# Sample attention's indexer, key and value pages: first loads issued in the last mixer steps, keys and values from two queues

## What is computed

```python
def dsa_sample(q, k, v, qi, ki, wi, cache_k, cache_v, cache_ki, page_table):
    ...
    ki_past = cache_ki[page_table].reshape(Bn, past, IDX_DIM).astype(ki.dtype)
    ki_all = jnp.concatenate([ki_past, ki], axis=1)
    ...
    score = index_scores(qi, wi, ki_all)
    score = jnp.where(kpos[None, None, :] <= qpos[None, :, None], score, -jnp.inf)
    _, top_i = lax.top_k(score, topk)
    ...
    kg = jnp.where(is_new, take(k, new_i), cache_k[phys, off].astype(k.dtype))
    vg = jnp.where(is_new, take(v, new_i), cache_v[phys, off].astype(v.dtype))
    return sparse_attend(q, kg, vg, valid)
```

## Time and profile before

| what | value |
|---|---|
| median of 3 runs (lowest, highest) | 4593.22 us (4589.61, 4599.74) |
| profiled execution, its own time | 4589.05 us |
| its span in the trace | 4587.4 us |
| PE, DVE, ACT, POOL busy | 81%, 47%, 23%, 12% |
| sample phase of layer 0, loading of `sel` to the end of its last store | 996.2 to 1326.7 us |
| the same of layer 1 | 3287.1 to 3618.0 us |

### The profile page before, as it was taken

One profiled execution on the slowest core, in us unless ns is written; L12 is line 12 of the kernel. 1 busy time (PEld: TensorE's weight loads), 2 busy tenths in 40 slices (PEclk: granted clock), 3 DMA queues, 4 the chain that ended last, 5 costly groups with the idle time before them and its releaser, 6 DMA issues.

```text
span 4587.4 us, 52594 instructions
## 1 busy us (share of the span) xinstructions
PE 3712.4 (81%) x17978; PEld 2757.6 (60%) x17978; DVE 2138.1 (47%) x4901; ACT 1037.1 (23%) x2273; POOL 546.9 (12%) x767
## 2 busy tenths in 40 slices
PE   5787778776638999999957787787766389999999
PEld 3555455553324899989835554554433248899898
DVE  1357788715503344344413577787155033443443
ACT  2322333223300211112022333332233002111120
POOL 0100100114120000100001000001141201001000
PEclk9888877556769999999978888775567699999999
DMA  3000000015331111111130000000153311111111
GB/s 121 19 13 14 14 10 8 7 29 168 98 130 60 46 37 56 37 37 56 44 120 20 12 13 15 10 8 7 30 170 96 128 60 47 37 56 37 37 56 49
DMA packets 165855, 230.68 MB, mean 50 GB/s; under 512 B 64562, under 2 KB 130164, under 8 KB 163540
## 3 DMA queue, kind: packets, MB, share of 16 engines
q1 hardware_dynamic: 139892, 166.03, 11.0%
q0 software_dynamic: 25696, 61.29, 4.4%
HBM read 203.74 MB, written 23.50 MB: 50 GB/s over the span
## 4 chain that ended last, share of the span: by engine, by line
PE 62%; issue 11%; DVE 10%; SPq 5%; ACT 4%; DVEq 2%; DMA 2%; POOLq 2%; POOL 1%; ACTq 0%
PE bank L1302 11%; PE bank L1303 11%; PE bank L1304 11%; PE bank L1012 9%; PE bank L1008 4%; PE bank L1110 3%; PE bank L1294 3%; DVE arena L1363 3%; SPq L455 2%; SPq L471 2%; ACT arena L642 1%; PE bank L1094 1%; POOLq L591 1%; DVE arena L1629 1%; SPq L424 1%
## 5 line engine op out<-in xcount | busy, mean ns | idle before, releaser
L1771 DVE TENSOR_TENSOR x_and_hraw<-x_and_hraw,bank 128x512 f32<-128x512 f32 (+1 forms) x576 | 396.4, 688 | 630.6 <-PE bank L1304 630.6
L642 ACT ACTIVATE arena<-bank 128x512 f32<-128x512 f32 (+11 forms) x926 | 356.2, 428 | 1112.6 <-PE bank L1012 335.8
L1012 PE MATMUL bank<-arena 128*128 128x512 f32 (+5 forms) x1440 | 526.3, 521 | 3.5 <-ACT arena L669 2.0
L1363 DVE TENSOR_SCALAR_CACHE_REDUCE arena<-arena,vectors 128x384 bf16<-128x384 f32 (+6 forms) x434 | 500.2, 1152 | 34.4 <-issue 2.5
L1302 PE MATMUL bank<-xT_hi,w_up_hi 128*128 128x364 f32 (+1 forms) x1536 | 506.7, 330 | 3.2 <-DVE vectors L1752 3.2
L1303 PE MATMUL bank<-xT_lo,w_up_hi 128*128 128x364 f32 (+1 forms) x1536 | 506.6, 330 | 0.0
L1304 PE MATMUL bank<-xT_hi,w_up_lo 128*128 128x364 f32 (+1 forms) x1536 | 506.5, 330 | 0.0
L1302 PE MATMUL bank<-w_down_hi,hidden_hi 128*128 128x512 f32 x1152 | 450.4, 391 | 7.5 <-issue 7.5
L1303 PE MATMUL bank<-w_down_lo,hidden_hi 128*128 128x512 f32 x1152 | 449.8, 390 | 0.0
L1304 PE MATMUL bank<-w_down_hi,hidden_lo 128*128 128x512 f32 x1152 | 449.6, 390 | 0.0
L1012 PEld LDWEIGHTS bank<-arena 128*128 128x128 f32 (+1 forms) x1440 | 254.4, 194 | 255.3 <-issue 225.4
(11 more groups left out here) (248 smaller groups left out, 4554.6 us busy)
## 6 DMA issues: line engine op xcount, KB each, us to landing
arena<-in_cache_k SPq DMA_DIRECT2D x256, 128.0 KB, 2.2
arena<-in_cache_v POOLq DMA_DIRECT2D x256, 128.0 KB, 2.4
w_up_landing<-in_w_up SPq DMA_DIRECT2D x32, 1024.0 KB, 7.5
w_down_landing<-in_w_down SPq DMA_DIRECT2D x32, 1024.0 KB, 4.9
arena<-in_w_in SPq DMA_DIRECT2D x16, 1322.0 KB, 17.6
out_projection<-in_w_out SPq DMA_DIRECT2D x16, 512.0 KB, 7.1
out_projection<-y_scratch SPq DMA_DIRECT2D x16, 512.0 KB, 3.6
y_scratch<-arena POOLq DMA_DIRECT2D x18, 256.0 KB
```

The costliest lines, as they stand in the source:

```text
L642: return act.activation(dst, src, ACT.Copy, scale=scale)
L1012: ins = mm(b[:R, o:o + w], xnT[:, c, 0:R], w_in[:, c, c0:c0 + w], start=c == 0, stop=c == 7)
L1363: ts(junk, sc, cf[:R].bitcast(F32), None, ALU.is_ge, ALU.add, accum_out=cnt[:R])
L1771: tt(x, x, b[P - R:P, :], ALU.add).then_inc(s_took, 1)
```

## The change

Per layer:

- `lgS` becomes the first area after `mixer_start`, and `kiraw`, now with a place for each of the 32 groups, lies on top of it. `Kraw` and `Vb` follow; `lgS`, `Kraw` and the first two slots of `Vb` end within the place of `w_in` (the assertion). `kiTc` shares its place with `KTc`.
- SP, before it meets the others at the mixer's end, waits for G3 of tile 8 and then issues 152 loads: all 128 indexer pages, key groups 0 and 2 (8 loads), and the values of the second sequence of pair 0 (16 loads). After the meeting it loads `sel`, the even key groups from 4 on (56 loads), and the second sequence's values of pairs 1 to 3 (48).
- POOL, in step 9, after the store of tile 6's attention output and before that of tile 7, issues 24 loads: key groups 1 and 3, and the values of the first sequence of pair 0. After the meeting: the odd key groups from 5 on (56) and the first sequence's values of pairs 1 to 3 (48).
- The instructions of PE, ACT and DVE and their order stay the same.

```diff
@@ -300,13 +300,14 @@
         top[0] = mixer_start
-        kiraw = area(4, 4, 64)
-        kiTc = area(2, 4, 512)
+        lgS = area(4, SW)
+        kiraw = view(lgS.rearrange("p a b -> p (a b)")[:, 0:4 * SB * 256], (4 * SB, 4, 64))
         Kraw = area(4, 4, 256)
+        Vb = area(4, NPAGE, 256)
+        assert top[0] - mixer_start - 2 * NPAGE * 256 <= 8 * NIN
         KTc = area(2, 4, 512)
-        Vb = area(4, NPAGE, 256)
+        kiTc = KTc
         rls = area(2, 512)
-        lgS = area(4, SW)
@@ -446,33 +447,45 @@
-                meet(sp, "sp")
-
-                sp.dma_start(sel, D["consts"][:, const_cols:all_cols]).then_inc(s_sel, 16)
                 sp.wait_ge(s_pt, 16 * (l + 1))
...
-                for n in range(0, 4 * SB, 2):
+
+                def load_k(n):
+
+                    bp, c, j = n // 8, n % 8 // 2, n % 2
+                    if n >= 4:
+                        o = n - 4
+                        sp.wait_ge(s_full_a, A_AT[l, "s", f"Kt{o // 8 * 5 + o % 8 // 2}.{2 * (o % 2) + 1}"] + 1)
+                    for k in range(4):
...
+                def load_v(bp):
+
+                    if bp >= 2:
+                        sp.wait_ge(s_pvs, l * 4 + bp - 1)
+                    q = 2 * (bp % 2) + 1
+                    for k in range(NPAGE):
...
+                sp.wait_ge(s_full_a, A_AT[l, NT, "G3"] + 1)
+                for n in range(4 * SB):
                     c, b = n // SB, n % SB
-                    if n >= 4:
-                        sp.wait_ge(s_full_a, A_AT[l, "s", f"kt{(n - 4) // 4}.{n % 4}"] + 1)
                     for k in range(4):
-                        sp.dma_start(kiraw[:, n % 4, k, :], D["cache_ki"][l, bass.ds(page(b, 4 * c + k), 1), :, :].rearrange("a p d -> (a p) d")
+                        sp.dma_start(kiraw[:, n, k, :], D["cache_ki"][l, bass.ds(page(b, 4 * c + k), 1), :, :].rearrange("a p d -> (a p) d")
                                      ).then_inc(s_kiraw[n % 4], 16)
...
+                load_k(0)
+                load_k(2)
+                load_v(0)
+                meet(sp, "sp")
+
+                sp.dma_start(sel, D["consts"][:, const_cols:all_cols]).then_inc(s_sel, 16)
+                for n in range(4, 32, 2):
+                    load_k(n)
+                for bp in range(1, 4):
+                    load_v(bp)
                 meet(sp, "sp")
@@ -550,6 +584,13 @@
                         stored(s_ybst)
+                    if s == TILES:
+
+                        pool.wait_ge(s_pt, 16 * (l + 1))
+                        pool.wait_ge(s_full_a, A_AT[l, NT, "G3"] + 1)
+                        load_k(1)
+                        load_k(3)
+                        load_v(0)
                     if s < TILES:
@@ -585,27 +626,9 @@
-                for n in range(1, 4 * SB, 2):
-                    c, b = n // SB, n % SB
-                    if n >= 4:
-                        pool.wait_ge(s_full_a, A_AT[l, "s", f"kt{(n - 4) // 4}.{n % 4}"] + 1)
...
-                for bp in range(4):
+                for n in range(5, 32, 2):
+                    load_k(n)
+                for bp in range(1, 4):
                     load_v(bp)
@@ -1195,7 +1218,7 @@
-                                ins = tr(b[0:64, k * P:(k + 1) * P], kiraw[:, q % 4, k, :], ident)
+                                ins = tr(b[0:64, k * P:(k + 1) * P], kiraw[:, q, k, :], ident)
```

More of the change, by code:

```diff
@@ L455, in page @@
                     return sp.value_load(ptab[0:1, b * NPAGE + n:b * NPAGE + n + 1], min_val=0, max_val=D["cache_k"].shape[1] - 1)
-                for n in range(0, 4 * SB, 2):
+                def load_k(n):
[4 more added lines that the diff above has]
+                    for k in range(4):
+                        sp.dma_start(Kraw[:, n % 4, k, :], D["cache_k"][l, bass.ds(page(2 * bp + j, 4 * c + k), 1)].rearrange("a p h d -> (a p) (h d)")
+                                     ).then_inc(s_Kraw[n % 4], 16)
@@ new lines, in load_v @@
+                def load_v(bp):
[3 more added lines that the diff above has]
+                    for k in range(NPAGE):
+                        sp.dma_start(Vb[:, q, k, :], D["cache_v"][l, bass.ds(page(2 * bp + 1, k), 1)].rearrange("a p h d -> (a p) (h d)")
+                                     ).then_inc(s_V[q], 16)
+                sp.wait_ge(s_full_a, A_AT[l, NT, "G3"] + 1)
+                for n in range(4 * SB):
@@ L457, in _ @@
                     c, b = n // SB, n % SB
-                    if n >= 4:
-                        sp.wait_ge(s_full_a, A_AT[l, "s", f"kt{(n - 4) // 4}.{n % 4}"] + 1)
                     for k in range(4):
-                        sp.dma_start(kiraw[:, n % 4, k, :], D["cache_ki"][l, bass.ds(page(b, 4 * c + k), 1), :, :].rearrange("a p d -> (a p) d")
+                        sp.dma_start(kiraw[:, n, k, :], D["cache_ki"][l, bass.ds(page(b, 4 * c + k), 1), :, :].rearrange("a p d -> (a p) d")
                                      ).then_inc(s_kiraw[n % 4], 16)
-                def load_k(bp):
-                    for n in range(8 * bp, 8 * bp + 8):
-                        c, j = n % 8 // 2, n % 2
-                        if n >= 4:
[L468 to L472, removed]
@@ L474, in _ @@
-                for bp in range(4):
-                    load_k(bp)
+                load_k(0)
[7 more added lines that the diff above has]
+                    load_v(bp)
                 meet(sp, "sp")
@@ L538, in y_part, with page, load_k, load_v @@
                     return y_scr[t].rearrange("p (c r) -> p c r", c=8)[:, c0:c0 + n, :]
+                def page(b, n):
+                    return pool.value_load(ptab[0:1, b * NPAGE + n:b * NPAGE + n + 1], min_val=0, max_val=D["cache_v"].shape[1] - 1)
+                def load_k(n):
+                    bp, c, j = n // 8, n % 8 // 2, n % 2
+                    if n >= 4:
+                        o = n - 4
+                        pool.wait_ge(s_full_a, A_AT[l, "s", f"Kt{o // 8 * 5 + o % 8 // 2}.{2 * (o % 2) + 1}"] + 1)
+                    for k in range(4):
+                        pool.dma_start(Kraw[:, n % 4, k, :], D["cache_k"][l, bass.ds(page(2 * bp + j, 4 * c + k), 1)].rearrange("a p h d -> (a p) (h d)")
+                                       ).then_inc(s_Kraw[n % 4], 16)
+                def load_v(bp):
+                    if bp >= 2:
+                        pool.wait_ge(s_pvs, l * 4 + bp - 1)
+                    q = 2 * (bp % 2)
+                    for k in range(NPAGE):
+                        pool.dma_start(Vb[:, q, k, :], D["cache_v"][l, bass.ds(page(2 * bp, k), 1)].rearrange("a p h d -> (a p) (h d)")
+                                       ).then_inc(s_V[q], 16)
                 rstd(0)
@@ L586, in _ @@
                 meet(pool, "pool")
-                pool.wait_ge(s_pt, 16 * (l + 1))
-                def page(b, n):
-                    return pool.value_load(ptab[0:1, b * NPAGE + n:b * NPAGE + n + 1], min_val=0, max_val=D["cache_v"].shape[1] - 1)
-                for n in range(1, 4 * SB, 2):
-                    c, b = n // SB, n % SB
-                    if n >= 4:
-                        pool.wait_ge(s_full_a, A_AT[l, "s", f"kt{(n - 4) // 4}.{n % 4}"] + 1)
[L596 to L608, removed]
+                for n in range(5, 32, 2):
+                    load_k(n)
+                for bp in range(1, 4):
                     load_v(bp)
```

## The result

The changed kernel takes 4402.78 us (median of 4 runs, 4399.42 to 4405.4); the kernel before, run beside it, 4595.67 (4 runs, 4589.61 to 4599.74). The ratio is 0.9581, with a 95% interval of 0.9564 to 0.9598: 193 us less. The forecast was 4386, 17 us lower; the range was 4368 to 4440. The profiled execution took 4405.4 us where its sum gave 4381.4: a gain of 183.7 instead of 207.6, so 24 us have to be found.

What follows compares the result with a forecast made beforehand. Load issue by SP and POOL was taken to bound the sample phase; 44 + 24.5 - 3 + 38.3 = 103.8 us a layer, 207.6 for both, gave 4381.4 for the profiled execution, 4386 for the median, range 4368 to 4440.

Steps and rivals of the forecast that it cites:

- The forecast's case: Sample phase: TensorE mostly at 2.4 GHz in the indexer part, 103.8 us gained a layer, 4386 us; chance 0.70.
- the forecast's own range: Whole kernel: 4368 to 4404 us, with small allowances on indexer part, masks, `sel` load, landings and mixer.
- The early loads: Mixer's end: SP's 152 loads hidden with 36 us to spare, POOL's 24 with 13 and 8; cost 0.
- Rival 4: Mixer's end: early loads delay the meeting; gain used up at 2.04 us a load, 4733 at 2.5; chance 0.01.
- Indexer part: Sample phase, first transposes to last score: 37 us instead of 81, 44 us a layer gained.
- Rival 1: Indexer part: TensorE stays at 1.2 GHz, 62 us instead of 37, total 4436; chance 0.15.
- Key part: Last score to the masks: the search ends last, 110.4 us for 134.9, 24.5 us a layer gained.
- Masks to pair 0: Masks until pair 0 ends: PE starts at 1.2 GHz but the clock rises; 3 us a layer lost (0 to 7).
- Values of pairs 2 and 3: Pair 0's end to PE's last products: 32 loads a queue, 40.7 us for 79.05, 38.3 us a layer gained.
- rival 3: Key and value loads: two queues together no faster than SP's 1.12 us a load, total 4533; chance 0.03.
- Tail: PE's last products to the store: 9.3 us, the same as before.
- Rival 2: Mixer's end: sample stores' landing doubles, POOL is late, the meeting slips by 39 us in all, total 4425; chance 0.10.

Runs made afterwards that it cites:

- experiment 3: The changed kernel with two more POOL drains a layer, behind its early loads and behind its last value loads: 4381.02 us.
- Experiment 5: The changed kernel with 20 of the search's 31 rounds, so the choice of keys is only approximate: 4337.67 us.
- experiment 6: The changed kernel with two more POOL drains a layer and 40 unused matmuls on PE ahead of the wait for the masks: 4365.3 us.
- Experiment 7: The changed kernel with all values on POOL again, keys still on two queues; POOL has 40 early loads, SP 136: 4507.24 us.
- Experiment 2: The kernel before, with keys and values split over SP and POOL and nothing loaded early: 4488.47 us.
- experiment 4: The changed kernel with 30 unused matmuls on PE ahead of the wait for the masks: 4401.06 us.
- experiment 1: The changed kernel with only the indexer pages early; keys all on SP, values all on POOL, after the meeting: 4498.44 us.

## Where the prediction held and where it did not

**What bounded the kernel, and the gain.** Held. From the first transposes to the store of `yTs` layer 0 went from 318.8 to 216.1 us, 102.7 less, where the sum had 103.8. The forecast's case is what happened. By the median 193 of 208 us came, near the bad end (4404) of the forecast's own range: two steps below were wrong by 24 us together, and 8 us came back where the sum was too careful.

**The early loads.** Hidden, as said, but with less to spare. SP's lasted until 975 instead of 956: 1.21 us each, not 1.12. SP's timeline shows the stretch of the indexer pages:

```profile
791.28 153.22 SPq L477 DMA_DIRECT2D arena<-in_cache_ki  x128
```

That is 1.20 us each, and SP's single issues took up to 4.7 us while POOL's sample stores landed (from 915 on). The meeting still didn't wait for SP. Rival 4 needed 2.04 us a load. POOL issued its 24 from 958.6 to 985.9, not by 979: layer 0's mixer ran 4 us late already (below), the wait for the stores' landing was 31.9 us for 29.7, and another 5.1 lay between tile 6's store and the first load. 10 of the 13 us of room were left.

**POOL's drains.** This step failed by omission: the sum had no term for them. It asked when POOL's loads would all be issued, and not what its entry into the meeting costs then, which grew with what POOL had issued. 2.0 + 4.6 = 6.6 us a layer over before, 13.1 in all; experiment 3 shows that they stand on the path. With the late mixer it also made the meeting 6 us later than the 996 that the prediction had as a sign of being wrong.

**Indexer part.** 35.0 for 37. TensorE ran at 0.91 of 2.4 GHz; the start at the low price was shorter than allowed. Rival 1 (62 us) fell. Here the rule of the Trainium skill (TensorE: Matmul & The Clock Gate, Part 1) held, that the clock doubles under sustained matmuls: it rose from 0.50 (1010.6 to 1016) to 0.92 (1016 to 1020). It doesn't explain the mixer's 34 us at 0.50, nor the 14.8 us of the masks.

**Key part.** 110.4 to the digit, and the keys were over at 1120, the values of pair 1 loaded when wanted. PE's wait for DVE was 36 us, more than the 15 to 30 expected, since at 0.91 its key work took less. Experiment 5 confirms that the search is the pace.

**Masks to pair 0.** The mechanism was seen, the size wrong: 8.5 us a layer, not 3, outside the 0 to 7. The step that failed is "but the clock rises on the way". Behind a pause it rose for no part of the 20 matmuls, in any kernel: 14.76 us, double the 7.52, and 13.81 behind the shortest pause. Experiments 2 to 5 and 7 show it, and experiment 6 that without the pause it is 7.52. 11 us in all.

**Values of pairs 2 and 3.** 39.9 for 40.7. Experiment 7 gives the other side, 78. Experiment 2 changed only the queues and gained 106 us, which rules out rival 3. The Trainium skill (DMA: Bandwidth & Descriptors, Issuing engines are not separate DMA queues) says that several issuing engines only save the sequencer's time, "usually small relative to the DMA itself". What was saved here is that time, and it was not small.

**Tail and mixer.** The tail was 1.4 us shorter. The mixer phases were longer: layer 0 reaches tile 7's store 4.1 us later, and from the store of `yTs` to tile 7's store of layer 1 it is 8.35 us more, of which the drain is 4.6. In layer 0 the 4 us are already there at 789.6, where G3 of tile 8 starts its last matmul (785.5 before), ahead of all that the change moves. SP's first early load starts with it, at 791.3 in the changed kernel and at 786.1 in experiments 3 and 6, whose code is the same up to there. Layer 1's stretch without its drain is 3.8 us longer than before, but 4.7 longer in experiment 2, which has no early loads, and 1.2 shorter in experiment 4, which has them all. So it isn't the loads' doing: single executions differ by as much (the kernel before by 10 us in four runs). Where the us come from stays open.

The 24 us of the two profiles are then: drains 13.1, masks 11, mixer 7.9; less 4 for the indexer part, 1.6 for the values and 2.8 for the tail makes 23.6 by layer 0's figures.

**Rival 2.** It didn't happen: no issue of POOL's delayed the meeting. Experiment 7 shows that a late POOL does delay it, by 16 us in layer 0 once it has 40 early loads. The landing of the sample stores, which rival 2 would have doubled, took 31.9 us, and 38.0 in experiment 7. The DMA engines' share of 0.02 that the prediction set against this rival is that of a stretch mostly behind the landing; while the stores landed (917 to 946) it was 0.09, and 1.38 in the changed kernel (921 to 952), beside SP's loads.

## What to carry to other kernels

Where the issue of loads and not their bytes sets the pace, a second issuing engine saves half of the issues' time; but count the queue's drain at the next barrier too, and let it drain early, while it would wait anyway. A speed-up that makes TensorE wait gives part of itself back: price the first work behind the new pause at the low clock, whole, as here the 20 matmuls of the masks. Filling such a pause pays only if hardly any of it is left: here 30 matmuls gave nothing, and 40 the whole 8.5 us a layer.

## What the runs showed of the chip that was not expected

- GpSimd's drain at a barrier takes time by what it has issued, even where everything has landed. In the meeting before the sample phase it took 1.77 us in the kernel before, 3.74 with 24 loads more and 5.04 with 40 more, 0.08 us a load; 0.13 if it has just drained. Behind the sample phase it is no plain count: 8.63 us for 105 DMAs of POOL, 8.30 for 153 (experiment 7), 5.69 and 4.06 for 193 (experiment 2, the kernel before), 4.06 for 129 (experiment 1). What a drain works off is open; no run was made for it.
- TensorE's clock was at 1.00 until a pause of 4.04 us and at 0.50 for all of the 14.8 us of dense matmuls behind it; pauses of 6.9 to 37 us cost the same, one of 2.15 us nearly the same (13.81 us), one of 0.7 us nothing. How long it stays down is not set by the pause: behind the 11.4 us for `sel` at the start of the changed sample phase it was at 0.50 for 9.6 us of nearly dense matmuls of other shapes, and up from 1016 on. What decides it is open.
- SyncE's issues stretched from 1.12 to 1.20 us on average (1.16 to 1.24 in the other kernels with early loads) while it issued beside the mixer's work, with single ones of 4.7 us while the sample stores were landing.
